# Splitting each 2 MB weight load of a two-block fp32 kernel into two 1 MB loads with a semaphore each

## The chip, the cores and the metric

The kernel runs on one core of a Trainium2 chip. The metric is the device time of one execution in microseconds (us), the median of several runs. Its engines run side by side and meet only at semaphores: PE is TensorE (PEld its weight loads), DVE is VectorE, ACT is ScalarE, POOL is GpSimd, SP is SyncE, which here only issues transfers. Sixteen DMA engines move all data between HBM and SBUF.

## What is computed

Two transformer blocks on 256 tokens of width 1024, all in fp32, batch 1. The first has adaptive modulation, a bidirectional retention with eight heads, a depthwise convolution branch, gates, and a mixture of 32 experts; the second has a gated MLP mixer, a sliding attention, gates and a mixture of 16 experts. Each token goes to two experts. Cut to what matters for the weights:

```python
mod = silu(c) @ w_ada + b_ada                          # 1024 x 6144
q, k, v, g, glu, gates = split(modulate(x) @ w_in + b_in)
ret = silu(g) * head_norm(retention(q, k, v))
y = sigmoid(ga) * (ret @ w_ret_out) + sigmoid(gb) * (conv_branch(glu) @ w_conv_out)
x = layernorm(ALPHA * x + gate * (y @ w_mix_out))
for e in range(32):                                    # 16 in the second block
    h = silu(t @ w_exp_gate[e]) * (t @ w_exp_up[e])    # 1024 x 512 each
    y = y + combine[:, e:e + 1] * (h @ w_exp_down[e])  # 512 x 1024
```

## The kernel before

All weights are cut on the host into blocks of 128 partitions by 4096 fp32 numbers, 16 KB in each partition, 2 MB in all (`BLK`, L41). One block (`kv2`) has half of that, 8 KB in each partition. A block holds a slice of the weights for the whole contraction: for a gate or up matrix and for most dense blocks, columns k*512 to (k+1)*512 of the tile are rows 128k to 128k+127 of the matrix, k from 0 to 7. So the first half of the tile's columns is the first half of the contraction. In a down block it is the first two of four k-tiles of 1024 columns, in `ret` blocks the first 8 of 16.

`make_jobs` (L80) lists every load in the order of use and gives each one of seven bays: three of a ring (`ring`), and four more large tensors (`RA`, `Vc`, `KQ`, `ZC`) that are free of other data in the expert stages. `ROUNDS` (L77) is the order of the bays in each stage: three bays in the dense stage of block one, seven for the experts. SP walks the list (`load`, L334 to L339): it waits until the last job on the block that lay in the bay before is done (`job_done`), and issues one DMA for the whole block, which adds 16 to the bay's semaphore `w_full`. SP's queue is in order.

PE takes the jobs in the same order. `job` (L682) does the dense ones: it waits for `w_full` of the bay (`w_wait`, L297) and for the pair of PSUM banks (`pair_free`), then issues the job's matmuls. The kinds differ in shape: `ada` has 8 matmuls, `cm8` has 4 chunks of 8 k-steps, `tm8` 2 chunks of 8. The first 4 of the 12 `ada` blocks open the kernel: each result goes to DVE (L1125), back through PE (`turn_ada`, L723) and to DVE again (L1106, which adds a slice of `vec` and frees the bank pair). After the fourth, ACT (L442) makes the modulated input `uT`, and the `glu` jobs (L701) begin. ACT issues its own loads meanwhile: `cin`, an early part of `const`, `vec` and the input `xT` at the start (L423 to L427), and after the second `ada` job the rest of `const`, `row`, the context `ctxT` and the router weights (L433 to L437). POOL loads rows of biases (L402).

In the expert stages (`route_and_experts`, L867 on) PE does three jobs for each expert: gate and up (`gate_or_up`, L930) with 16 matmuls of 256 columns each, and down (L945) with 8 of 512 columns. Between them it turns the hidden values and scatters the last expert's output (L920). A matmul in fp32 stands in the trace as two. Thirty experts of block one and fourteen of block two are taken in this static way. The last two, and any second windows of experts with many tokens, run in a loop whose length depends on the data (`Fori`): their loads are issued by `last_experts` (L341, issues at L350 and L357) into three bays with semaphores of their own, `wg_full`, `wu_full`, `wd_full`.

Of the kernel before, what the change touches and what calls it, by code (L numbers as in the profile page):

```python
# [26 lines left out]
ALU = mybir.AluOpType  # L27
# [89 lines left out]
def build(nc, a):  # L117
# [3 lines left out]
    with ExitStack() as ctx:  # L121
# [115 lines left out]
        ld_c, ld_first, ld_rest, ld_x, ld_ctx, ld_wr = (sem(n) for n in ("ld_c", "ld_first", "ld_rest", "ld_x", "ld_ctx", "ld_wr"))  # L237
        w_full = [sem(f"w_full{i}") for i in range(BAYS)]
        job_done = sem("job_done")
# [29 lines left out]
        for n in range(2):  # L269
            moe.append({k: sem(f"{k}{n}") for k in (  # L270
                "logits", "logits_kept", "logits_turned", "gexp_in", "eexp_in", "gexp_out", "eexp_out", "hot_ready", "ranks",
                "items_ready", "u_turned", "u_rows", "diag_ready", "bc_ps", "bc_kept", "wg_full", "wu_full",
                "wd_full", "g_ready", "gathered", "x_kept", "xs_ready", "gate_done", "up_done", "down_done",
                "sg_ready", "hid_ready", "ht_ps", "ht_ready", "y_kept", "s_ready", "scattered", "acc_done", "step")})
# [21 lines left out]

        def w_wait(eng, w):  # L297

            eng.wait_ge(w_full[loads[w]["bay"]], 16 * (loads[w]["nth"] + 1))

# [30 lines left out]
        def _(sp):  # L331
            def load(w):

                x = loads[w]  # L334
                if x["prev"] is not None:
                    sp.wait_ge(job_done, last_of[x["prev"]] + 1)
                s = a["w_" + x["src"]]
                bay = bays[x["bay"]]
                sp.dma_start(bay[:, 0:s.shape[2]], s[x["b"]]).then_inc(w_full[x["bay"]], 16)  # L339

# [80 lines left out]
        def _(act):  # L421
# [154 lines left out]
            def route_and_experts(n):  # L576
# [9 lines left out]
                ins.then_inc(m["u_rows"], 1)  # L586
                act.wait_ge(m["gexp_in"], 1)
                nc.scalar.activation(r_("gd"), r_("gd"), ACT.Exp).then_inc(m["gexp_out"], 1)
                act.wait_ge(m["eexp_in"], 1)
                nc.scalar.activation(r_("e2"), r_("e2"), ACT.Exp).then_inc(m["eexp_out"], 1)  # L590

# [88 lines left out]
        def _(pe):  # L680
            def job(j):

                w_wait(pe, j["w"])
                if j["use"]:
                    pe.wait_ge(pair_free[j["pair"]], j["use"])
                W, out, kind = W_of(j), PP[j["pair"]], j["kind"]
                if kind == "ada":

                    for k in range(DT):
                        at = 32 * (k % 4)  # L690
                        ins = pe.matmul(out[at:at + 32, 0:2, :].rearrange("p a n -> p (a n)"), sT[:, k, :],  # L691
                                        W[:, k * 512:(k + 1) * 512], start=k < 4, stop=k >= 4, tile_position=(0, at))
                elif kind in ("cm8", "cm4", "cm16"):
# [4 lines left out]
                    for c in range(2 if K == 16 else 4):  # L698
                        at = c * P + (512 * j["half"] if K == 4 else 0)
                        for k in range(K):  # L700
                            ins = pe.matmul(out[:, c, :], W[:, k * width + at:k * width + at + P], X[:, k, :],  # L701
                                            start=k == 0, stop=k == K - 1)
                elif kind in ("tm8", "tm8c"):
                    X = ucT if kind == "tm8c" else uT
                    for t in range(LT):
                        for k in range(DT):
                            ins = pe.matmul(out[:, 2 * t:2 * t + 2, :].rearrange("p a n -> p (a n)"),  # L707
                                            X[:, k, t * P:(t + 1) * P], W[:, k * 512:(k + 1) * 512], start=k == 0,
                                            stop=k == DT - 1)
                elif kind == "kv":  # L710
                    for k in range(DT):
                        pe.matmul(out[:, 0, :], W[:, k * 256:k * 256 + P], uT[:, k, :], start=k == 0, stop=k == DT - 1)
                    for t in range(LT):
                        for k in range(DT):
                            ins = pe.matmul(out[:, 2, t * P:(t + 1) * P], uT[:, k, t * P:(t + 1) * P],
                                            W[:, k * 256 + P:(k + 1) * 256], start=k == 0, stop=k == DT - 1)
# [150 lines left out]
            def route_and_experts(n):  # L867
# [56 lines left out]

                def gate_or_up(q, W, x, early=None):
                    for k in range(DT):
                        if early is not None and k % 4 == 0:
                            pe.wait_ge(m["x_kept"], early + k // 4)
# [11 lines left out]

                def down(k, W):
                    pe.wait_ge(m["ht_ready"], k + 1)
                    for c in range(4):
                        for g in range(2):
                            ins = pe.matmul(bank[2][SLOTS * g:SLOTS * (g + 1), :],  # L945
                                            hts[:, c % 2, SLOTS * (c // 2):SLOTS * (c // 2 + 1)],
                                            W[:, c * D + g * 512:c * D + (g + 1) * 512], start=c == 0, stop=c == 3,
                                            tile_position=(0, SLOTS * g))
# [7 lines left out]
                for k in range(E - 2):  # L956
                    jg, ju, jd = (J[f"moe{n}", 3 * k + q, 0] for q in range(3))
                    if k:
                        pe.wait_ge(m["xs_ready"], k)
                    w_wait(pe, jg["w"])  # L960
                    gate_or_up(0, W_of(jg), xs if k else xsc[:, :, 0:SLOTS], None if k else 1).then_inc(job_done, 1)
                    if k == 0:

# [11 lines left out]
                        pe.matmul(flat(MB[3]), ys[:, 0:P], ys, start=True, stop=False)  # L975
                    w_wait(pe, ju["w"])
                    gate_or_up(1, W_of(ju), xs if k else xsc[:, :, 0:SLOTS]).then_inc(job_done, 1)
                    if k:
# [6 lines left out]
                    else:  # L985
                        pe.wait_ge(m["bc_kept"], 1)
                    w_wait(pe, jd["w"])
                    down(k, W_of(jd)).then_inc(job_done, 1)
                wg, wu, wd = (bays[x] for x in tail_bays(n))
# [101 lines left out]
        def _(dve):  # L1091
# [260 lines left out]
            def route(n):  # L1352
# [21 lines left out]
                say(dve, V_.tensor_tensor(t2("gd", GROUPS), lt[:, :, 0:GROUPS], r_("gm").unsqueeze(2).to_broadcast([P, LT, GROUPS]),  # L1374
                                          ALU.subtract), m["gexp_in"], 1)
                first_of(t2("hg", GROUPS), lt[:, :, 0:GROUPS], r_("gm"), GROUPS)
# [10 lines left out]
                link(V_.tensor_reduce(r_("m2"), ml, AX.X, ALU.max))  # L1387
                say(dve, V_.tensor_tensor(r_("e2"), r_("m2"), r_("m1"), ALU.subtract), m["eexp_in"], 1)
                first_of(t2("h2", EG), ml, r_("m2"), EG)
# [5 lines left out]

                dve.wait_ge(m["gexp_out"], 1)
                link(V_.tensor_reduce(r_("gw"), t2("gd", GROUPS), AX.X, ALU.add))
                dve.wait_ge(m["eexp_out"], 1)
                link(V_.scalar_tensor_tensor(r_("w1"), r_("e2"), 1.0, r_("gw"), ALU.add, ALU.mult))
# [329 lines left out]
```

## Time and profile before

| | |
|---|---|
| median of 3 runs | 1634.03 us (1631.02 to 1635.21) |
| the profiled execution | 1630.79 us |
| its span, first to last instruction | 1629.0 us |
| PE busy | 1534.9 us, 94% |
| weight loads (PEld) | 1021.2 us, 63% |
| DVE busy | 492.4 us, 30% |
| ACT busy | 213.7 us, 13% |
| moved by DMA | 435.54 MB, 267 GB/s over the span |
| mean granted TensorE clock | 0.988 of full speed |

The rows in the next section are in microseconds from the first instruction, unless marked ns. A slice of the page is a fortieth of the span, 40.7 us. For a DMA issue, the last number is the time from the issue to the landing of the last byte.

### The profile page before, as it was taken

How to read it: one execution, taken by the hardware profiler on the slowest of the kernel's cores; microseconds unless marked ns; L12 is line 12 of the kernel's file. 1: busy time of each engine (PE TensorE's matmuls, PEld its weight loads, DVE VectorE, ACT ScalarE, POOL GpSimd, SP SyncE). 2: the span in 40 equal slices, each digit the busy share in tenths (PEclk: the TensorE clock that was granted, in tenths of full speed). 3: DMA queues.
4: the chain of work that ended last, by engine and by line, in shares of the span. 5: the costliest groups of instructions: out<-in, count | busy, mean ns of one | idle time of the engine just before them, and what ended most of it. 6: DMA issues, size and time to landing. Idle time of an engine off the chain costs nothing.

```text
span 1629.0 us, 20472 instructions
## 1 busy us (share of the span) xinstructions
PE 1534.9 (94%) x8922; PEld 1021.2 (63%) x8922; DVE 492.4 (30%) x1080; ACT 213.7 (13%) x385; POOL 16.9 (1%) x37
## 2 busy tenths in 40 slices
PE   5999999999999999999998998889999899999996
PEld 2876644674688888555545554547788787555544
DVE  1546686453101117112111111115023133212113
ACT  1100100121112003211111001102022022111102
POOL 0000000000000001000000000000000000000000
PEclk7999999999999999999999999999999999999999
DMA  9523222464433564799999999994544543999994
GB/s 393 197 103 117 104 66 108 169 251 168 150 140 124 193 249 147 286 426 427 427 426 427 425 427 427 427 406 192 142 181 155 207 155 144 426 428 425 427 422 179
DMA packets 33469, 435.54 MB, mean 267 GB/s; under 512 B 4049, under 2 KB 5593, under 8 KB 7145
## 3 DMA queue, kind: packets, MB, share of 16 engines
q1 hardware_dynamic: 29376, 423.64, 64.0%
q10 hardware_dynamic: 2328, 6.15, 1.5%
q0 software_dynamic: 1680, 4.52, 0.8%
q8 instruction: 67, 1.10, 0.3%
q14 instruction: 18, 0.14, 0.0%
HBM read 431.67 MB, written 2.62 MB: 267 GB/s over the span
## 4 chain that ended last, share of the span: by engine, by line
PE 75%; DMA 18%; DVE 3%; ACT 1%; issue 0%; DVEq 0%; SPq 0%; ACTq 0%
PE PP L701 25%; PE PP L930 14%; PE PP L707 13%; PE PP L945 7%; DMA RA<-in_w_moe 6%; DMA ring<-in_w_moe 6%; PE MB L920 4%; DMA Vc<-in_w_moe 4%; DMA ZC<-in_w_moe 2%; PE PP L911 2%; PE MB L849 1%; PE PP L691 1%; PE MB L792 1%; PE MB L774 1%; PE MB L795 1%; PE PP L938 1%
## 5 line engine op out<-in xcount | busy, mean ns | idle before, releaser
L701 PE MATMUL PP<-uT,ring 128*128 128x256 f32 x1088 | 239.4, 382 | 3.7 <-ACT uT L442 2.7
L701 PEld LDWEIGHTS PP<-uT,ring 128*128 128x128 f32 x1088 | 208.0, 192 | 34.4 <-ACT uT L442 2.8
L930 PE MATMUL PP<-ring,const 128*64 128x256 f32 x1312 | 148.8, 380 | 11.5 <-DMA ring<-in_w_moe 10.6
L930 PEld LDWEIGHTS PP<-ring,const 128*64 128x64 f32 x1312 | 98.2, 137 | 68.9 <-DMA ring<-in_w_moe 16.5
L707 PE MATMUL PP<-ring,uT 128*128 128x512 f32 x288 | 125.0, 592 | 0.0
L1477 DVE TENSOR_SCALAR V<-V 128x1 f32<-128x1 f32 x50 | 7.7, 154 | 372.8 <-PE PP L930 372.8
L1164 DVE SCALAR_TENSOR_TENSOR ZC<-ZC,vec 128x256 f32<-128x256 f32 x240 | 116.4, 485 | 8.6
L920 PE MATMUL MB<-V 64*128 64x256 f32 x800 | 112.9, 401 | 1.7 <-DVE V L1488 1.7
L707 PEld LDWEIGHTS PP<-ring,uT 128*128 128x128 f32 x288 | 54.5, 190 | 67.0 <-issue 67.0
L920 PEld LDWEIGHTS MB<-V 64*128 64x128 f32 x800 | 69.1, 186 | 34.5 <-issue 30.0
L707 PE MATMUL PP<-ring,RA 128*128 128x512 f32 x192 | 83.4, 592 | 0.0
L1483 DVE SCALAR_TENSOR_TENSOR V<-V 128x256 f32<-128x256 f32 x100 | 48.5, 485 | 93.0 <-PE MB L920 91.2
L930 PE MATMUL PP<-RA,const 128*64 128x256 f32 x544 | 62.2, 381 | 10.6 <-DMA RA<-in_w_moe 10.2
L945 PE MATMUL PP<-ring,const 128*64 128x512 f32 x304 | 69.4, 598 | 0.0
L607 ACT ACTIVATE V<-PP 128x256 f32<-128x256 f32 x50 | 19.2, 384 | 380.6 <-PE PP L930 380.6
L1488 DVE COPY V<-PP 128x512 f32<-128x512 f32 x50 | 34.6, 692 | 107.2 <-PE PP L945 107.2
L707 PEld LDWEIGHTS PP<-ring,RA 128*128 128x128 f32 x192 | 36.5, 190 | 45.1 <-issue 45.0
L930 PEld LDWEIGHTS PP<-RA,const 128*64 128x64 f32 x544 | 39.4, 137 | 34.9 <-DMA RA<-in_w_moe 13.8
L611 ACT ACTIVATE const<-small 128x512 f32 x50 | 31.8, 636 | 194.5 <-PE PP L930 194.5
L701 PE MATMUL PP<-Vc,ring 128*128 128x256 f32 x256 | 55.6, 379 | 0.0
L930 PE MATMUL PP<-KQ,const 128*64 128x256 f32 x448 | 51.0, 380 | 3.4 <-DMA KQ<-in_w_moe 3.2
L701 PEld LDWEIGHTS PP<-Vc,ring 128*128 128x128 f32 x256 | 48.6, 190 | 6.6
(310 smaller groups left out, 1568.1 us busy)
## 6 DMA issues: line engine op xcount, KB each, us to landing
ring<-in_w_moe SPq DMA_DIRECT2D x61, 2048.0 KB, 23.1
RA<-in_w_moe SPq DMA_DIRECT2D x25, 2048.0 KB, 20.9
ZC<-in_w_moe SPq DMA_DIRECT2D x25, 2048.0 KB, 21.7
KQ<-in_w_moe SPq DMA_DIRECT2D x20, 2048.0 KB, 24.6
Vc<-in_w_moe SPq DMA_DIRECT2D x19, 2048.0 KB, 23.4
ring<-in_w_ada SPq DMA_DIRECT2D x12, 2048.0 KB, 8.7
ring<-in_w_gates SPq DMA_DIRECT2D x7, 2048.0 KB, 8.7
ring<-in_w_v SPq DMA_DIRECT2D x5, 2048.0 KB, 8.4
```

The source lines that it names most:

```text
L607: nc.scalar.activation(sg, bank[0][:, 0:L], ACT.Silu).then_inc(m["sg_ready"], 1)
L611: nc.scalar.activation(xs, xsc[:, :, bass.ds(at, SLOTS)], ACT.Copy).then_inc(m["xs_ready"], 1)
L691: ins = pe.matmul(out[at:at + 32, 0:2, :].rearrange("p a n -> p (a n)"), sT[:, k, :], W[:, k * 512:(k + 1) * 512], start=k < 4, stop=k >= ...
L701: ins = pe.matmul(out[:, c, :], W[:, k * width + at:k * width + at + P], X[:, k, :], start=k == 0, stop=k == K - 1)
L707: ins = pe.matmul(out[:, 2 * t:2 * t + 2, :].rearrange("p a n -> p (a n)"), X[:, k, t * P:(t + 1) * P], W[:, k * 512:(k + 1) * 512], start ...
L911: ins = pe.matmul(out[:, (k % 4) * P:(k % 4 + 1) * P], Kct[:, t, k * P:(k + 1) * P], G[:, c, t, :], start=t == 0, stop=t == 1)
L920: ins = pe.matmul(MB[k // 2][:, k % 2, :], ys[g, (k % 4) * P:(k % 4 + 1) * P], S[g, :], start=False, stop=done == "acc_done" and k % 2 == ...
L930: ins = pe.matmul(bank[q][SLOTS * g:SLOTS * (g + 1), 0:L], x[:, k, :], W[:, k * 512 + g * 256:k * 512 + (g + 1) * 256], start=k == 0, stop ...
L945: ins = pe.matmul(bank[2][SLOTS * g:SLOTS * (g + 1), :], hts[:, c % 2, SLOTS * (c // 2):SLOTS * (c // 2 + 1)], W[:, c * D + g * 512:c * D ...
L1164: ins = V_.scalar_tensor_tensor(conv[:, t, :], zpad[:, t, k:k + L], tap, conv[:, t, :], ALU.mult, ALU.add)
L1483: linked(V_.scalar_tensor_tensor(Sk[:, c], placer[:, c], slotcol, weightr[:, c], ALU.is_equal, ALU.mult), k, c + 2)
L1488: V_.tensor_copy(ys, bank[2]).then_inc(m["y_kept"], 1)
```

## The change

Each block is loaded by two DMAs, one for each half of its columns, and each half has a semaphore of the bay. So a DMA moves 8 KB in each partition, out of rows that lie 16 KB apart in HBM. Every job waits for the first half ahead of its first matmul, and for the second half ahead of the first matmul that reads it, which is the middle of the contraction of its first chunk. The loads of the last experts (`last_experts`) stay whole. To make room for the seven new semaphores, four semaphores of each router are joined to two: `gexp_in` and `eexp_in` become `exp_in` with the values 1 and 2, and the same for `exp_out`.

```diff
-        w_full = [sem(f"w_full{i}") for i in range(BAYS)]
+        w_first = [sem(f"w_first{i}") for i in range(BAYS)]
+        w_second = [sem(f"w_second{i}") for i in range(BAYS)]
...
-        def w_wait(eng, w):
+        def first_half(eng, w):
 
-            eng.wait_ge(w_full[loads[w]["bay"]], 16 * (loads[w]["nth"] + 1))
+            eng.wait_ge(w_first[loads[w]["bay"]], 16 * (loads[w]["nth"] + 1))
+
+        def second_half(eng, w):
+
+            eng.wait_ge(w_second[loads[w]["bay"]], 16 * (loads[w]["nth"] + 1))
...
-                sp.dma_start(bay[:, 0:s.shape[2]], s[x["b"]]).then_inc(w_full[x["bay"]], 16)
+                whole, part = s.shape[2], s.shape[2] // 2
+                sp.dma_start(bay[:, 0:part], s[x["b"], :, 0:part]).then_inc(w_first[x["bay"]], 16)
+                sp.dma_start(bay[:, part:whole], s[x["b"], :, part:whole]).then_inc(w_second[x["bay"]], 16)
...
-                w_wait(pe, j["w"])
+                first_half(pe, j["w"])
...
                         for k in range(K):
+                            if c == 0 and k == K // 2:
+                                second_half(pe, j["w"])
                             ins = pe.matmul(out[:, c, :], W[:, k * width + at:k * width + at + P], X[:, k, :],
                                             start=k == 0, stop=k == K - 1)
...
-                def gate_or_up(q, W, x, early=None):
+                def gate_or_up(q, W, x, early=None, w=None):
                     for k in range(DT):
+                        if w is not None and k == 4:
+                            second_half(pe, w)
...
-                def down(k, W):
+                def down(k, W, w=None):
                     pe.wait_ge(m["ht_ready"], k + 1)
                     for c in range(4):
+                        if w is not None and c == 2:
+                            second_half(pe, w)
...
-                act.wait_ge(m["gexp_in"], 1)
-                nc.scalar.activation(r_("gd"), r_("gd"), ACT.Exp).then_inc(m["gexp_out"], 1)
-                act.wait_ge(m["eexp_in"], 1)
-                nc.scalar.activation(r_("e2"), r_("e2"), ACT.Exp).then_inc(m["eexp_out"], 1)
+                act.wait_ge(m["exp_in"], 1)
+                nc.scalar.activation(r_("gd"), r_("gd"), ACT.Exp).then_inc(m["exp_out"], 1)
+                act.wait_ge(m["exp_in"], 2)
+                nc.scalar.activation(r_("e2"), r_("e2"), ACT.Exp).then_inc(m["exp_out"], 1)
```

The other kinds of dense jobs (`ada`, `tm8`, `kv`) get the same wait at the middle of their k loop, the calls in the expert stages pass the load's number, and DVE's four lines that speak of the joined semaphores follow.

## Rows read from the trace of the kernel before

**Rows 1.** The page's slices of the span: GB/s.
```profile
GB/s 393 197 103 117 104 66 108 169 251 168 150 140 124 193 249 147 286 426 427 427 426 427 425 427 427 427 406 192 142 181 155 207 155 144 426 428 425 427 422 179
```

**Rows 2.** The chain of work that ended last: start, length, what.
```profile
427.87 13.82 PE PP L701 x64
...
518.53 55.27 PE PP L701 x256
...
814.86 30.56 DMA ZC<-in_w_moe
...
1086.38 11.26 DMA RA<-in_w_moe
...
1589.41 10.79 DMA RA<-in_w_moe
```

**Rows 3.** A stretch: length, busy PE, PEld, DVE, ACT, POOL, then PEclk, DMA share, GB/s.
```profile
814.00:1098.00 284.00, 256.32 (x1874) 142.10 (x1872) 50.62 (x114) 27.03 (x58) 0.00 (x0) 1.00 1.00 424
```

**Rows 4.** Two of SP's issues, windows of the DMA view: KB, us to landing.
```profile
Vc<-in_w_moe SPq DMA_DIRECT2D x1, 2048.0 KB, 8.2
...
ZC<-in_w_moe SPq DMA_DIRECT2D x1, 2048.0 KB, 9.8
```

**Rows 5.** Timeline of SP: the issues of rows 4 and 6.
```profile
668.51 0.33 SPq L339 DMA_DIRECT2D Vc<-in_w_moe  x1
...
1093.88 0.44 SPq L339 DMA_DIRECT2D ring<-in_w_q  x1
1094.36 0.53 SPq L339 DMA_DIRECT2D Vc<-in_w_kv  x1
...
1378.95 0.33 SPq L339 DMA_DIRECT2D ZC<-in_w_moe  x1
```

**Rows 6.** A 2 MB block and the 1 MB block queued right behind it.
```profile
ring<-in_w_q SPq DMA_DIRECT2D x1, 2048.0 KB, 23.4
Vc<-in_w_kv SPq DMA_DIRECT2D x1, 1024.0 KB, 25.4
```

**Rows 7.** DMA queues from 21.9 to 29.3: packets, MB, share of 16 engines.
```profile
q1 hardware_dynamic: 142, 2.06, 65.6%
q10 hardware_dynamic: 142, 1.09, 35.4%
```

**Rows 8.** Loads of the start, windows of the DMA view: KB, us to landing.
```profile
hT<-in_xT ACTq DMA_DIRECT2D x1, 1024.0 KB, 27.2
...
ring<-in_w_ada SPq DMA_DIRECT2D x1, 2048.0 KB, 15.0
...
ring<-in_w_glu SPq DMA_DIRECT2D x1, 2048.0 KB, 18.3
const<-in_const ACTq DMA_DIRECT2D x1, 1476.0 KB, 18.5
```

**Rows 9.** Timeline of the start: transfers issued (start of the first, length of all).
```profile
0.73 13.74 SPq L339 DMA_DIRECT2D ring<-in_w_ada  x4
...
2.14 1.11 ACTq L427 DMA_DIRECT2D hT<-in_xT  x1
...
19.28 15.61 SPq L339 DMA_DIRECT2D ring<-in_w_glu  x3
```

**Rows 10.** Timeline of the start: work, and in brackets the idle time before.
```profile
10.39 0.22 ACT L430 ACTIVATE sT<-cin 128x16 f32<-128x16 f32 x1 [5.76 <-DMA cin<-in_cT]
...
16.33 2.91 PE L691 MATMUL PP<-ring,sT 128*32 128x512 f32 x16 [2.26 <-DMA ring<-in_w_ada]
...
21.97 1.42 DVE L1125 COPY small<-PP 128x512 f32<-128x512 f32 x2 [21.97 <-DMA vec<-in_vec]
...
25.13 3.64 PE L691 MATMUL PP<-ring,sT 128*32 128x512 f32 x16 [0.49 <-DVE modT L1106]
...
31.06 3.45 PE L691 MATMUL PP<-ring,sT 128*32 128x512 f32 x16 [0.48 <-DVE modT L1106]
...
39.13 1.22 PE L701 MATMUL PP<-uT,ring 128*128 128x256 f32 x2 [2.71 <-ACT uT L442]
```

More of the change, by code:

```diff
@@ L270, in build @@
             moe.append({k: sem(f"{k}{n}") for k in (
-                "logits", "logits_kept", "logits_turned", "gexp_in", "eexp_in", "gexp_out", "eexp_out", "hot_ready", "ranks",
+                "logits", "logits_kept", "logits_turned", "exp_in", "exp_out", "hot_ready", "ranks",
                 "items_ready", "u_turned", "u_rows", "diag_ready", "bc_ps", "bc_kept", "wg_full", "wu_full",
@@ L689, in job @@
                     for k in range(DT):
+                        if k == DT // 2:
+                            second_half(pe, j["w"])
                         at = 32 * (k % 4)
@@ L700, in job @@
                         for k in range(K):
+                            if c == 0 and k == K // 2:
+                                second_half(pe, j["w"])
                             ins = pe.matmul(out[:, c, :], W[:, k * width + at:k * width + at + P], X[:, k, :],
@@ L706, in job @@
                         for k in range(DT):
+                            if t == 0 and k == DT // 2:
+                                second_half(pe, j["w"])
                             ins = pe.matmul(out[:, 2 * t:2 * t + 2, :].rearrange("p a n -> p (a n)"),
@@ L711, in job @@
                     for k in range(DT):
+                        if k == DT // 2:
+                            second_half(pe, j["w"])
                         pe.matmul(out[:, 0, :], W[:, k * 256:k * 256 + P], uT[:, k, :], start=k == 0, stop=k == DT - 1)
@@ L959, in route_and_experts @@
                         pe.wait_ge(m["xs_ready"], k)
-                    w_wait(pe, jg["w"])
-                    gate_or_up(0, W_of(jg), xs if k else xsc[:, :, 0:SLOTS], None if k else 1).then_inc(job_done, 1)
+                    first_half(pe, jg["w"])
+                    gate_or_up(0, W_of(jg), xs if k else xsc[:, :, 0:SLOTS], None if k else 1, jg["w"]).then_inc(job_done, 1)
                     if k == 0:
@@ L975, in route_and_experts @@
                         pe.matmul(flat(MB[3]), ys[:, 0:P], ys, start=True, stop=False)
-                    w_wait(pe, ju["w"])
-                    gate_or_up(1, W_of(ju), xs if k else xsc[:, :, 0:SLOTS]).then_inc(job_done, 1)
+                    first_half(pe, ju["w"])
+                    gate_or_up(1, W_of(ju), xs if k else xsc[:, :, 0:SLOTS], w=ju["w"]).then_inc(job_done, 1)
                     if k:
@@ L986, in route_and_experts @@
                         pe.wait_ge(m["bc_kept"], 1)
-                    w_wait(pe, jd["w"])
-                    down(k, W_of(jd)).then_inc(job_done, 1)
+                    first_half(pe, jd["w"])
+                    down(k, W_of(jd), jd["w"]).then_inc(job_done, 1)
                 wg, wu, wd = (bays[x] for x in tail_bays(n))
@@ L1374, in route @@
                 say(dve, V_.tensor_tensor(t2("gd", GROUPS), lt[:, :, 0:GROUPS], r_("gm").unsqueeze(2).to_broadcast([P, LT, GROUPS]),
-                                          ALU.subtract), m["gexp_in"], 1)
+                                          ALU.subtract), m["exp_in"], 1)
                 first_of(t2("hg", GROUPS), lt[:, :, 0:GROUPS], r_("gm"), GROUPS)
@@ L1387, in route @@
                 link(V_.tensor_reduce(r_("m2"), ml, AX.X, ALU.max))
-                say(dve, V_.tensor_tensor(r_("e2"), r_("m2"), r_("m1"), ALU.subtract), m["eexp_in"], 1)
+                say(dve, V_.tensor_tensor(r_("e2"), r_("m2"), r_("m1"), ALU.subtract), m["exp_in"], 2)
                 first_of(t2("h2", EG), ml, r_("m2"), EG)
@@ L1394, in route @@
                 say(dve, V_.tensor_tensor(t2("M", E), A[:, 0], A[:, 1], ALU.add), m["hot_ready"], 1)
-                dve.wait_ge(m["gexp_out"], 1)
+                dve.wait_ge(m["exp_out"], 1)
                 link(V_.tensor_reduce(r_("gw"), t2("gd", GROUPS), AX.X, ALU.add))
-                dve.wait_ge(m["eexp_out"], 1)
+                dve.wait_ge(m["exp_out"], 2)
                 link(V_.scalar_tensor_tensor(r_("w1"), r_("e2"), 1.0, r_("gw"), ALU.add, ALU.mult))
```

## The prediction

> **What bounds the kernel now.** I read the page's slices first. PE is busy nearly everywhere, but the transfers have two plateaus at 422 to 428 GB/s, slices 18 to 26 and 35 to 39, and far less outside [rows 1]. A plateau at one height is a limit, so the next question is who sets the end in it. The chain of waits answers: it runs over PE until 814.86, and from there steps on weight transfers, 30 us long at first, come again and again to the end of block one's experts; block two's experts end the same way [rows 2]. In the table of stretches, 814 to 1098 has a DMA share of 1.00 at 424 GB/s, and PE idles 28 us [rows 3].
>
> The point to see is that the transfers set the end of each expert stage from well before 814. A transfer issued at 668.51 lands 8.2 us later [rows 4, 5], and a block takes 2.097 MB / 424 GB/s = 4.95 us, so it already stood behind another. PE has prefetched blocks and so does not feel it until it has eaten them. But the last block lands when all bytes since 668 have been moved, whatever PE does. It lands at 1086.38 + 11.26 = 1097.64 [rows 2]. Block two does the same from the transfer that was issued at 1378.95 and landed at 1388.7 [rows 4, 5], to 1589.41 + 10.79 = 1600.2 [rows 2]. Elsewhere PE sets the pace and loads have slack, but for the first 39 us, where loads, DVE and PE take turns [rows 10].
>
> So the change has two prices that can show: what a block costs the DMA engines in the two full stretches, and what happens in the first 39 us.
>
> **Part 1: the waits it shortens in the expert stages.** PE can start a gate job 2.45 us sooner once the first half has landed. It then stops at the middle for the second half. The wait is about 1 us a block and there were 28 us of it from 814 to 1098 [rows 3]. It is worth nothing at the end: the transfer ahead does not come sooner, because the queue is never empty (share 1.00, and 30 us from issue to landing, six blocks deep [rows 2, 3]). The last experts' loads, the ones that do end the stage, stay whole and have their old waits. Gain 0.
>
> **Part 2: the price of smaller packets.** A block is 128 rows of 16 KB, and becomes 256 rows of 8 KB and a second round of semaphore writes. The trace has two rows with 8 KB pieces. The lower bound is `kv2`, 1 MB from the same queue right behind `q2`: they land at 1094.36 + 25.4 = 1119.76 and 1093.88 + 23.4 = 1117.28 [rows 5, 6], 2.48 us for 1 MB with times rounded to 0.1. The same bytes at 424 GB/s take 2.47. With the rounding, two such halves cost between 0 and 0.1 us more than a whole block; I take 0.03 as the low end. The upper bound is from 21.9 to 29.3, where ACT's queue q10 moves `xT` in 8 KB pieces beside q1's 16 KB pieces. q1 spends 0.656 * 16 * 7.4 / 2.06 = 37.7 us of one engine on a MB, q10 0.354 * 16 * 7.4 / 1.09 = 38.5 [rows 7]. The difference of 0.8 us a MB is 0.8 * 2.097 / 16 = 0.10 us a block, 0.13 if the last digit of the shares falls badly. I take 0.06, nearer to `kv2`, since that row is of the same queue and back to back.
>
> How many blocks pay? In block one, from the landing at 668.51 + 8.2 = 676.7 to 1097.64 there are 421 us, 85 blocks at 4.95, with the first 86; five of these are whole ones of the last experts, so 81. In block two, 211.5 us are 43 blocks, 11 of them whole, so 32. 113 * 0.06 = +6.8 us; the ends give 113 * 0.03 = 3.4 and 113 * 0.13 = 14.7. Before 668, and between the stages, the loads are asked for long ahead and the price is hidden by PE's own work.
>
> The Trainium skill (DMA: Bandwidth & Descriptors, section Bandwidth) speaks against the change: its table has 1 MB transfers at 6.15 us, 78% of peak, and asks for at least 1 MiB. By that figure, with nothing overlapped, 226 halves would add 226 * (6.15 - 2.48), some 830 us; this trace disagrees, since the 1 MB block passes in 2.48 us. The same section's paragraph on small descriptors gives 3 cycles of 850 MHz for each packet: an estimate from it is 8 * 3.5 ns = 0.03 us a block and a total of +3.2 us, the low end above.
>
> **Part 3: the start.** At the start the two queues take turns packet by packet, and not by bytes. ACT's queue has `cin`, `const`, `vec` and `xT`, each in 128 rows. The small `cin` lands at 10.39 and the small `vec`, two places on, only at 21.97, though SP's second `ada` block is there at 16.33 [rows 10]: that is one place of ACT's queue for each block of SP's. `xT` (1 MB) lands at 2.14 + 27.2 = 29.3 with SP's fourth block (0.73 + 13.74 + 15.0 = 29.5), and the rest of `const` at 19.3 + 18.5 = 37.8 with the first `glu` block, 19.28 + 18.3 = 37.6 [rows 8, 9]. With 8 KB pieces on SP's queue, an ACT transfer will land with one half of a block, so SP's share falls. 1 MB is 2.45 us. Taking it out of each step (10.4, then 5.9, 5.6 and 7.4 us): `cin` 7.9, `const` and the whole first block 11.5, `vec` 14.7 with half of the second block, `xT` and the second block 19.7 (before 16.33). PE ends the second `ada` job 1.7 us (its last four k-steps) later, 21.4 (before 16.33 + 2.91 = 19.2 [rows 10]). That job releases ACT's second set of loads. `vec` no longer holds the turn, so the third job starts at 23.8 (before 25.13) and ends near 27.4 (before 28.8). But from 23.5, about 2 us after ACT's issues, the third and fourth blocks share the engines with 1.48 MB of `const`, then `row` and `ctxT`. Half a block beside `const` takes the step from 29.5 to 37.6 less 2.45, 5.7 us, where before the fourth block had only `xT` beside it. The halves of the third block land at 22.2 and 25.5, those of the fourth near 30.5 and 34.4. So the fourth job ends at 34.4 + 1.7 = 36.1 (before 31.06 + 3.45 = 34.5), and 4.6 us later the `glu` jobs start, at 40.7 (before 39.13). The first `glu` block's second half lands near 41.5 to 42, after its first four k-steps (1.7 us), which adds little. I take +2.0 us. Bounds: -1.5, if ACT's loads do not delay the fourth block (third job 1.3 us sooner, and all behind it); +4, if the first `glu` block is late as well. The shift passes whole through the PE-bound stretch and into both expert stages.
>
> **Part 4: what costs nothing.** Sixty dense jobs get a wait in the middle that is already met. The waits met at the head of a job show no cost: one `cm8` job is 13.82 us, and four in a row 55.27 [rows 2]; at most 0.01 each, 0.6 in all. SP issues twice as often, 0.33 to 0.53 us each [rows 5], two within 4.95 us, and with nothing else on its queue but loads. Behind a PE wait in the middle stand only that job's own matmuls. The joined semaphores count the same two events on ACT and DVE in the same order: 0.
>
> **Sum.** 0 + 6.8 + 2.0 + 0 = +8.8 us. The profiled execution took 1630.79 us around its span of 1629.0 and would take 1639.6; it stands 3.2 us under the median, so the median goes from 1634.0 to 1642.8, call it 1643 (+0.54%). About 0.3%, 4.9 us, is what a measurement of this kernel can tell from no change.
>
> **The rivals.**
> *The packets are almost free.* 0.03 us a block or less and a start of 0 to +1: 1634 + 3.4 + 0.5 = 1638, a change that can't be told. For it speaks `kv2`; against it the dearer 8 KB pieces of rows 7 and the extra semaphore writes. Chance 0.22.
> *The shorter waits pay.* If SP's issues, and not the engines, held the stream, PE's earlier release of a bay (up to 1.8 us, half a job) would move every later transfer. It would take back PE's idle time: 28 us in 814 to 1098 and, scaled by length to the 75 us that end block two's experts, 7 more: at most 1634 - 35 + 2 = 1601, and it decides as soon as the DMA share between 700 and 1098 is under 1.00 by more than 4.9 / 430 of it. The share of 1.00 and the 30 us in the queue are against it [rows 2, 3]. Chance 0.10, with smaller gains of any kind in it.
> *Small transfers cost more than a packet's share.* With 12 or 14 transfers in flight instead of 6 or 7 the engines may lose time between them, or the 16 KB stride reads slower from HBM; the trace has no such row. A transfer that met one other in the queue landed in 8.2 us where its bytes need 4.95 [rows 4]; if a tenth of that 3.2 showed for each added transfer, it would be 113 * 0.32 = +36, and 1634 + 36 + 2 = 1672. Chance 0.08. (The table of the Trainium skill cited in part 2, DMA: Bandwidth & Descriptors, Bandwidth, points this way.)
> *The forecast.* 1643, its own range 1638.5 to 1649. Chance 0.60.
>
> **How the numbers follow.** The range leaves out the large gain, the 1672 case and slivers, and takes in the free packets and both bounds of part 2: 1631 to 1650. Slower: 0.60 less a sliver, 0.08, and a fifth of the first rival: 0.68. Same: 0.21. Faster: 0.11.
>
> **What would show it.** In the changed profile: the plateaus at 420 to 423 GB/s where they had 424 to 427, the share still 1.00; the `glu` jobs starting at 40 to 42 with `vec` landed near 15 and the second `ada` block near 20; PE's waits for DMA more in number and shorter; last landing of block one some 8 us after 1097.64. It would be wrong if the plateaus keep their height, if they fall below 418, or if the DMA share in them drops under 1.

## The result and the profile after

The changed kernel takes 1645.14 us in the median of 4 runs (1641.72 to 1647.64), the kernel before 1632.85 us in the median of its 4 (1631.02 to 1635.21; one run more than in the table above). The ratio is 1.0077, 95% interval 1.0060 to 1.0093: slower, by more than the 0.3% that a measurement of this kernel can tell. The profiled execution took 1641.72 us around a span of 1639.9, against 1630.79 and 1629.0: +10.9 us on either count.

The page's slices of the changed kernel, GB/s, and two rows of its queues and issues:

```profile
GB/s 387 199 103 116 103 66 107 171 249 163 153 150 108 205 256 125 308 419 420 420 421 420 420 420 420 420 405 200 155 166 154 205 154 154 421 419 420 422 417 182
...
q1 hardware_dynamic: 55872, 423.65, 64.4%
...
ring<-in_w_moe SPq DMA_DIRECT2D x114, 1024.0 KB, 24.7
```

The plateaus stand where they stood, but their height is 417 to 422 GB/s instead of 422 to 428 [rows 1]. The load of one block has become two issues of 1 MB, and queue q1 has 55872 packets for the 29376 of before, for the same 424 MB.

The chain of waits of the changed kernel (start, length, what):

```profile
1026.22 29.91 DMA RA<-in_w_moe
...
1094.71 11.21 DMA RA<-in_w_moe
...
1600.31 10.84 DMA RA<-in_w_moe
```

The last up block of block one lands at 1094.71 + 11.21 = 1105.92, where it was 1097.64; that of block two at 1611.15, where it was 1600.20 [rows 2]. The start of the changed kernel, in its timeline:

```profile
10.56 1.93 PE L700 MATMUL PP<-ring,sT 128*32 128x512 f32 x8 [2.36 <-DMA ring<-in_w_ada]
...
14.00 1.93 PE L700 MATMUL PP<-ring,sT 128*32 128x512 f32 x8 [1.51 <-DMA ring<-in_w_ada]
14.17 0.69 DVE L1144 COPY small<-PP 128x512 f32<-128x512 f32 x1 [14.17 <-DMA vec<-in_vec]
...
18.97 1.93 PE L700 MATMUL PP<-ring,sT 128*32 128x512 f32 x8 [3.04 <-DMA ring<-in_w_ada]
...
29.11 1.94 PE L700 MATMUL PP<-ring,sT 128*32 128x512 f32 x8 [0.48 <-DVE modT L1125]
...
32.92 1.94 PE L700 MATMUL PP<-ring,sT 128*32 128x512 f32 x8 [1.88 <-DMA ring<-in_w_ada]
34.79 3.58 PE L738 MATMUL PP<-const,small 128*128 128x2 f32 x16
...
41.07 9.29 PE L712 MATMUL PP<-uT,ring 128*128 128x256 f32 x31 [2.71 <-ACT uT L449]
```

An `ada` job is now two groups of 8 matmuls. `vec` lands at 14.17 (21.97 before), but the second half of the second block only at 18.97 (the whole at 16.33 before), and the fourth job stands in its middle for a half that lands at 32.92. The `glu` jobs begin at 41.07 instead of 39.13 [rows 10].

With three events in each trace (first `glu` matmul, last up block of block one, last up block of block two) the loss can be placed: 1.94 us up to the first event, 1064.85 - 1058.51 = 6.34 us from the first to the second, 505.23 - 502.56 = 2.67 us from the second to the third. These are called the start, the first stretch and the second stretch below. The sum is 10.95 us, all of the profile's difference. The 113 split blocks that stand in a full queue pay 9.0 / 113 = 0.080 us each.

This is one pair of executions. How far another pair could differ is read from the others: with whole blocks in the expert stages the first stretch took 1057.41 to 1058.87 us in five kernels (the one before and four of the experiments below), so differences of up to 1.5 us in it say nothing.

### The profile page after: what moved, and what is told of

The parts are those of the page before. It is cut to its first block, busy times and chain, and to the rows that moved or that the text cites. A ratio compares the mean times of both kernels' runs of the same rounds, so it can differ in the third digit from the quotient of the medians.

```text
span 1639.9 us, 20658 instructions
## 1 busy us (share of the span) xinstructions
PE 1544.3 (94%) x8922; PEld 1013.8 (62%) x8922; DVE 492.0 (30%) x1080; ACT 213.6 (13%) x385; POOL 16.7 (1%) x37
## 3 DMA queue, kind: packets, MB, share of 16 engines
q1 hardware_dynamic: 55872, 423.65, 64.4%
q10 hardware_dynamic: 2328, 6.15, 1.5%
## 4 chain that ended last, share of the span: by engine, by line
PE 70%; DMA 24%; DVE 3%; SPq 1%; ACT 1%; issue 1%; DVEq 0%; ACTq 0%
PE PP L712 25%; PE PP L720 13%; DMA RA<-in_w_moe 12%; PE PP L947 11%; PE PP L964 5%; DMA KQ<-in_w_moe 3%; DMA ring<-in_w_moe 3%; PE MB L935 3%; DMA ring<-in_w_ada 2%; PE PP L926 2%; DMA Vc<-in_w_moe 2%; DMA ZC<-in_w_moe 2%; PE MB L864 1%; PE PP L700 1%; PE MB L807 1%; PE MB L789 1%
## 5 line engine op out<-in xcount | busy, mean ns | idle before, releaser
L947 PE MATMUL PP<-ring,const 128*64 128x256 f32 x1312 | 152.2, 381 | 12.7 <-DMA ring<-in_w_moe 12.5
L947 PEld LDWEIGHTS PP<-ring,const 128*64 128x64 f32 x1312 | 93.9, 137 | 76.5 <-DMA ring<-in_w_moe 27.0
```

The source lines that it names most:

```text
L947: ins = pe.matmul(bank[q][SLOTS * g:SLOTS * (g + 1), 0:L], x[:, k, :], W[:, k * 512 + g * 256:k * 512 + (g + 1) * 256], start=k == 0, stop ...
```

## The experiments

The first question was what in a split block costs 0.08 us: its smaller packets, the second transfer, or the 16 KB stride in HBM. The second was whether the start is a separate cost. The third came from the rival of the shorter waits. All edits are against the changed kernel, except the last experiment's.

**Halves contiguous in HBM.** The static experts' weights come from a second copy.

```diff
-                sp.dma_start(bay[:, 0:part], s[x["b"], :, 0:part]).then_inc(w_first[x["bay"]], 16)
-                sp.dma_start(bay[:, part:whole], s[x["b"], :, part:whole]).then_inc(w_second[x["bay"]], 16)
+                h = a["h_" + x["src"]]          # [block, 2, 128, 2048]; dense blocks keep the two lines above
+                sp.dma_start(bay[:, 0:part], h[x["b"], 0]).then_inc(w_first[x["bay"]], 16)
+                sp.dma_start(bay[:, part:whole], h[x["b"], 1]).then_inc(w_second[x["bay"]], 16)
...
+        d[f"h_moe{n}"] = np.ascontiguousarray(s.reshape(3 * E, P, 2, BLK // 2).transpose(0, 2, 1, 3))
```

> The expert blocks of the static experts are loaded in two transfers as in the changed kernel, but from a second copy of the weights in which each half lies contiguous in HBM (8 KB rows behind one another), so the 16 KB stride is gone and all else is as in the changed kernel. In the changed kernel the first glu job starts at 41.07 (before 39.13), the last up block of block one lands at 1105.92 (before 1097.64) and that of block two at 1611.15 (before 1600.20): 1.94 us are lost at the start, 6.35 in block one's expert stage and 2.66 in block two's, 9.0 for 113 blocks, 0.080 us each. Theory packets (each packet and each semaphore write has a fixed price): landings within 0.7 us of 1105.9 and 1611.2. Rival stride (HBM reads at a 16 KB pitch are slower): landings near 1099.6 and 1602.2, a gain of 9 us on the changed kernel. Rival transfers (each DMA has a price, or the issue that SP is held in): as theory packets.

Measured: 1644.51 us, ratio 1.0075 (1.0054 to 1.0097), plateaus at 420 GB/s, `glu` jobs from 41.53, landings at 1107.00 and 1614.96. The first stretch is 1065.47 us, as in the changed kernel and not 6 us less. The stride costs nothing that can be seen. The landings are 1.1 and 3.8 us past the changed kernel's, more than the 0.7 that was forecast: the `glu` jobs began 0.5 us later, and of the second difference 2.7 us arise in PE's middle stage, where the granted clock fell (below).

**Halves by partitions, lower and upper.**

```diff
-                sp.dma_start(bay[:, 0:part], s[x["b"], :, 0:part]).then_inc(w_first[x["bay"]], 16)
-                sp.dma_start(bay[:, part:whole], s[x["b"], :, part:whole]).then_inc(w_second[x["bay"]], 16)
+                sp.dma_start(bay[0:half, 0:whole], s[x["b"], 0:half, :]).then_inc(w_first[x["bay"]], 16)
+                sp.dma_start(bay[half:P, 0:whole], s[x["b"], half:P, :]).then_inc(w_second[x["bay"]], 16)
```

> Two transfers of 1 MB again with a semaphore each, but cut by partitions: rows 0 to 63 and rows 64 to 127, 16 KB in each. PE waits for both ahead of a job. Number of transfers, semaphore writes and SP's issues as in the changed kernel, packets as in the kernel before. Theory packets: the two expert stages cost 0 to 1.5 us together (113 semaphore writes an engine), the glu jobs start at 38 to 39.5, span 1629 to 1631. Rival transfers: the stages cost 9.0 us, span near 1638. Rival stride: 0.

Measured: 2226.43 us, ratio 1.3663 (1.3578 to 1.3749). Every theory missed this one. Its row of 900 to 1000, with the columns of rows 3:

```profile
900.00:1000.00 100.00, 61.37 (x344) 35.11 (x344) 9.24 (x22) 5.49 (x12) 0.00 (x0) 0.80 1.01 218
```

The DMA engines are busy all the time (1.01) and move 218 GB/s, half. So transfers into one half of the partitions keep all engines busy and get half of the rate, and this experiment says nothing about the price of a transfer as such. The even and odd partitions, below, took its place.

**Only the start split, and all but the start.** In the first, the condition below; in the second, `w >= 8`. PE's wait for the second half has the same condition.

```diff
+                if w < 8:
                     sp.dma_start(bay[:, 0:part], s[x["b"], :, 0:part]).then_inc(w_first[x["bay"]], 16)
                     sp.dma_start(bay[:, part:whole], s[x["b"], :, part:whole]).then_inc(w_second[x["bay"]], 16)
+                else:
+                    sp.dma_start(bay[:, 0:whole], s[x["b"]]).then_inc(w_first[x["bay"]], 16)
```

> Only the first eight loads (four ada, four glu) are split, all others are whole as before. Theory (at the start the queues take turns by packets, so ACT's large loads take more of the engines beside 8 KB packets and the fourth ada block is late): glu jobs start at 41.1, both expert stages cost 0, span 1631 (+1.9), time +0.12%. Rival (the start in the changed profile was the clock or chance, and all 10.9 us are the stages): glu jobs start at 39.1, span 1629.

> The complement: the first eight loads are whole, all later ones split. Theory: glu jobs start at 39.1, stages cost 6.35 + 2.66 = 9.0 us, span 1638, time +0.55%. Rival: the whole 10.9 us, span 1640.

Measured, start only: 1634.66 us, ratio 1.0020 (1.0010 to 1.0030), `glu` jobs from 41.47, first stretch 1057.41 (none of the 6.3 us), plateaus back at 427 GB/s. Its span is 1633.0 and not 1631, for the second stretch is 505.38 although no block in it is split. Measured, all but the start: 1643.03 us, ratio 1.0066 (1.0043 to 1.0090), first stretch 1064.97, span 1640.3 and not 1638; here too the second stretch is long, 508.32. So the two parts are separate and come near to the whole.

The start of this second version was forecast at 39.1, as in the kernel before, and began 0.9 us earlier:

```profile
30.96 1.92 PE L706 MATMUL PP<-ring,sT 128*32 128x512 f32 x16 [0.48 <-DVE modT L1131]
...
38.20 6.10 PE L718 MATMUL PP<-uT,ring 128*128 128x256 f32 x15 [3.40 <-DMA ring<-in_w_glu]
```

Its first eight loads are the ones of the kernel before. But its fourth `ada` job took 1.92 us at a granted clock of 1.00, where the kernel before took 3.45 at 0.53 [rows 10], and PE then waited for the first `glu` block. So the kernel before had a slow start in its profile, and the price of the start is not fixed: 1.9 us against that profile, about 3 against this one.

What else the forecasts missed by is the middle of the second stretch. Its windows from 1180 to 1230, of the kernel before, of the start-only kernel, of the changed one and of its complement:

```profile
1180.00:1230.00 50.00, 47.29 (x270) 41.95 (x269) 11.70 (x17) 11.30 (x14) 4.47 (x8) 1.00 0.50 189
```
```profile
1180.00:1230.00 50.00, 47.29 (x256) 41.75 (x255) 11.69 (x17) 11.30 (x14) 4.39 (x8) 0.93 0.45 169
```
```profile
1180.00:1230.00 50.00, 47.29 (x268) 41.86 (x267) 11.69 (x17) 9.30 (x12) 4.29 (x8) 1.00 0.50 186
```
```profile
1180.00:1230.00 50.00, 47.29 (x253) 41.63 (x252) 11.70 (x17) 9.20 (x11) 4.28 (x8) 0.93 0.44 167
```

The granted clock is 1.00 in the kernel before and in the changed one, and 0.93 in the two experiments: around the attention, where PE has waits for DVE between its jobs, the clock falls to 1.2 GHz for a moment in some executions. In the start-only kernel it averages 0.65 from 1210 to 1215, and PE gets through 16 matmuls there and not 25. With it goes 2.8 us (505.38 against 502.56, both with whole blocks in the second stretch). Corrected by that, the complement's second stretch is 508.32 - 2.8 = 505.5, as in the changed kernel. The correction is itself rough: the last experiment below has whole blocks, reads 0.93 too, and took 507.38. The first stretch has no such stage, and its spread is 1.5 us, so the verdicts below go by it.

**One transfer, small packets.** 2 MB in one DMA with one semaphore, but 8 KB pieces, for the static experts; the dense blocks are whole, in 16 KB pieces.

```diff
+                    sp.dma_start(bay.rearrange("p (h n) -> p h n", h=2), h[x["b"]].rearrange("h p n -> p h n")
+                                 ).then_inc(w_first[x["bay"]], 16)
```

> One transfer of 2 MB for each block with one semaphore, as before, but the static experts' blocks come from the copy with the halves apart in HBM, so that each packet is 8 KB: 256 packets a transfer. Packets of the changed kernel without its second transfer. Stage costs are read between events inside a run: from the first glu matmul to the landing of the last up block of block one (1058.51 before, 1064.85 changed), and from there to the landing of the last up block of block two (502.56 and 505.23; these hold PE's middle stage, where a dip of the granted clock can add 2 to 3 us). Theory packets: most of the price stays, 1063.5 to 1064.8 us in the first stretch, since only one semaphore write in 18 goes. Rival transfers: 1058.5. SP's issues fall back to 0.3 to 0.5 us in either case.

Measured: 1640.62 us, ratio 1.0068 (1.0042 to 1.0095), first stretch 1101.62 - 37.90 = 1063.72, plateaus at 420 GB/s. Of the 6.3 us in this stretch 5.2 are there with half of the transfers; the 1.1 that are missing are within the spread. The `glu` jobs began at 37.90, with whole blocks at the start as in the version above. The forecast on SP was wrong: its issues did not fall back to 0.5 us (one of them, of `KQ` at 1015.23, took 3.15), see the last section.

**Even and odd partitions.** The counterpart: two transfers, two semaphores, 16 KB packets, PE waiting for both.

```diff
+                sp.dma_start(bay[0:P:2, 0:whole], s[x["b"], 0:P:2, :]).then_inc(w_first[x["bay"]], 16)
+                sp.dma_start(bay[1:P:2, 0:whole], s[x["b"], 1:P:2, :]).then_inc(w_second[x["bay"]], 16)
```

> Two transfers of 1 MB and two semaphores as in the changed kernel, PE waiting for both, each of 64 rows of 16 KB, but the even and the odd partitions instead of the lower and the upper half, where the rate had halved (217 GB/s). Theory A, each transfer covers every part of SBUF and the rate is back: with 16 KB packets the first stretch is 1058.5 to 1060 and the plateaus are at 424 to 427 GB/s, against 1064.9 if the price were one of transfers. Theory B, any transfer of 64 rows is slow: near 217 GB/s and 2200 us as with the halves of partitions.

Measured: 1636.71 us, ratio 1.0030 (1.0016 to 1.0044), first stretch 1099.62 - 40.26 = 1059.36. Theory A: the rate is back at 427 GB/s, and 81 added transfers cost at most 0.85 us, 0.01 each, which the spread of 1.5 us does not tell from nothing. The rest of its 3.8 us is the start (+1.1) and the second stretch (+1.8, clock 0.97 there). The stretch 900 to 1000 in four kernels, first the one with one transfer and 8 KB packets, then even and odd, then the changed kernel, then quarters:

```profile
900.00:1000.00 100.00, 88.06 (x654) 49.83 (x652) 16.68 (x37) 8.80 (x19) 0.00 (x0) 1.00 1.01 420
```
```profile
900.00:1000.00 100.00, 89.61 (x664) 53.48 (x661) 16.87 (x39) 8.96 (x20) 0.00 (x0) 1.00 1.01 427
```
```profile
900.00:1000.00 100.00, 91.28 (x646) 46.75 (x644) 17.97 (x40) 8.81 (x19) 0.00 (x0) 0.98 1.01 420
```
```profile
900.00:1000.00 100.00, 87.54 (x638) 44.64 (x632) 16.68 (x37) 8.82 (x19) 0.00 (x0) 1.00 1.03 409
```

The last number is what the reader is to see: 420 with one transfer or with two, as long as the packets are 8 KB, and 427 with two transfers of 16 KB packets. The packets make the price.

One rival is left by this comparison: in the changed kernel, with one transfer of 8 KB pieces and with quarters, SP was also held at its issues (last section), and in the even and odd one it was not. The changed kernel's own trace decides it. From 683 to 764 all its issues took 0.33 to 1.05 us, and the rate was already down, here from 680 to 760, first before, then changed:

```profile
680.00:760.00 80.00, 80.00 (x604) 44.40 (x602) 16.53 (x37) 8.44 (x18) 0.00 (x0) 1.00 1.01 427
```
```profile
680.00:760.00 80.00, 80.00 (x600) 44.09 (x598) 16.89 (x38) 8.44 (x18) 0.00 (x0) 1.00 1.01 420
```

**Quarters.** The suspected cost tripled.

```diff
+                for i in range(4):
+                    n = s.shape[2] // 4
+                    sp.dma_start(bay[:, i * n:(i + 1) * n], s[x["b"], :, i * n:(i + 1) * n]
+                                 ).then_inc((w_first, w_second)[i // 2][x["bay"]], 16)
```

> The suspected cost tripled: every static block in four transfers of 512 KB, 4 KB in each partition, the first two on the first semaphore and the last two on the second (32 in each wait). Theory packets: 24 packets and 3 semaphore writes more an engine than before, where the change had 8 and 1, so three times its 0.080 us a block: +0.24 * 81 = +19 in the first stretch (1078) and +0.24 * 32 = +8 in the second (510). The start gets worse as well, since ACT's transfers then land with a quarter of a block each: glu jobs at 42 to 45. Span near 1660. Rival, a price by transfer or by SP's issue that only shows when SP is held: more than four times, span over 1675.

Measured: 1667.96 us, ratio 1.0234 (1.0208 to 1.0260). First stretch 1122.61 - 45.62 = 1076.99 (forecast 1078), second 512.79 (forecast 510), `glu` jobs from 45.62 (forecast 42 to 45). 409 GB/s is 5.13 us a block, 420 is 4.99 and 427 is 4.91: 8 more packets and one more semaphore write an engine cost 0.08 us, 24 and 3 cost 0.22. So a packet, with its share of a semaphore write, costs about 9 to 10 ns of an engine on top of its bytes.

**PE waits for both halves.** The early start on the first half is taken away.

```diff
         def first_half(eng, w):
             eng.wait_ge(w_first[loads[w]["bay"]], 16 * (loads[w]["nth"] + 1))
+            eng.wait_ge(w_second[loads[w]["bay"]], 16 * (loads[w]["nth"] + 1))
...
         def second_half(eng, w):
-            eng.wait_ge(w_second[loads[w]["bay"]], 16 * (loads[w]["nth"] + 1))
+            pass
```

> The changed kernel's transfers, but PE waits for both halves ahead of a job, so the early start on the first half is taken away. Theory (the early start is worth nothing where transfers set the pace, and at the start only the fourth ada job's half, 1.9 us): first stretch 1064.9 as changed, last landings where they were but for the start, glu jobs at 42 to 43.5, span 1641 to 1643. Rival (the shorter waits paid, and the price of transfers is larger than 9 us): span over 1650.

Measured: 1644.57 us, ratio 1.0081 (1.0059 to 1.0104), the changed kernel's. `glu` jobs from 41.92, first stretch 1065.53, span 1642.8. PE's waits for the ring's blocks from 814 to 1098 (in total, times, longest), before, changed, and with both halves waited for:

```profile
PE PP L930 <- DMA ring<-in_w_moe: 10.6, 11, 1.1
```
```profile
PE PP L947 <- DMA ring<-in_w_moe: 10.4, 24, 0.6
```
```profile
PE PP L948 <- DMA ring<-in_w_moe: 13.2, 14, 2.2
```

For the ring's blocks the split halves the longest wait and doubles the number. Over all bays the sum of PE's waits for blocks is 26.1 us before, 27.0 with the split and 31.1 with both halves waited for, and the longest with the split is 2.1, one for `RA`. The end of the stage stays in all of them where the stream puts it.

**Three blocks split, ACT's loads later.** What the runs point to: split only where small packets help, at the start, and keep ACT's large loads away from the fourth `ada` block. The first of the three versions is below; the other two also issue `xT` after the third `ada` job, and the last of them has no split at all.

```diff
+                if w < 3:
                     sp.dma_start(bay[:, 0:part], s[x["b"], :, 0:part]).then_inc(w_first[x["bay"]], 16)
...
-            job_wait(act, J["ada", 1, 0])
+            job_wait(act, J["ada", 3, 0])
             act.dma_start(const[:, early:], a["const"][:, early:]).then_inc(ld_rest, 16)
```

> A version made from what the runs show: only the first three ada blocks are split, since there the 8 KB packets let ACT's small loads through (vec at 14.2 where it was 22.0); the fourth and all others are whole; and ACT's second set of loads (const's rest, row, ctxT, router weights) is issued after the fourth ada job, not the second, so that nothing delays the fourth block. Theory: fourth ada block lands near 29, glu jobs start at 37.3 (before 39.13), or up to 1 us off with the granted clock; expert stages as before; span 1627, time -0.1%. Rival (the context load becomes late for ACT and delays the glu results' way out of PSUM): glu jobs start at 37.3 but 1 to 3 us are lost before 111; span 1629 to 1631.

> As e9, and the input xT (1 MB) is issued after the third ada job, not at the start: it is needed only for the first glu job. Theory: ada blocks land 2.4 us sooner, glu jobs start near 35, span 1625, time -0.25%. Rival (xT lands beside the first glu block and becomes what the glu jobs wait for): glu jobs start at 37 or later.

> The control to e10: the kernel before with all blocks whole and the same two delays of ACT's loads. Theory (with 16 KB packets vec still lands with the third ada block, near 22, and the turn of the first ada result waits for it): glu jobs start at 38.5 to 39.1, time within 0.1% of before. Rival (the delays alone do the work, the split nothing): glu jobs start near 35 to 36.

First `glu` matmul of the three:

```profile
36.03 24.22 PE L718 MATMUL PP<-uT,ring 128*128 128x256 f32 x99 [2.71 <-ACT uT L455]
```
```profile
38.12 22.24 PE L719 MATMUL PP<-uT,ring 128*128 128x256 f32 x93 [4.20 <-ACT uT L456]
```
```profile
41.45 18.90 PE L702 MATMUL PP<-uT,ring 128*128 128x256 f32 x78 [7.65 <-ACT uT L443]
```

The first starts the `glu` jobs 3.1 us earlier than the kernel before (and 1.9 to 2.2 earlier than the two versions with whole blocks above) and keeps it to the last up block of block one (1094.27 against 1097.64). In its profile the clock in the middle stage was 0.93 and the second stretch 505.33 us instead of 502.56, which took 2.8 of it: span 1628.4, and 1630.69 us against 1631.62, ratio 1.0006 (0.9994 to 1.0018). That is no difference. The second fell to its rival: `xT`, issued at 23.9, is 12.0 us under way beside SP's blocks and holds ACT to 35.99; 1630.52 us, ratio 1.0001 (0.9990 to 1.0012). In the third, with whole blocks, it lands at 39.24 and costs 2.3 us; 1635.44 us, ratio 1.0024 (1.0011 to 1.0038). Neither its theory (38.5 to 39.1, time unchanged) nor its rival came true: the `glu` jobs wait for the late `xT`, which lands 3.3 us later than in the second version. No version that was run beats the kernel before by what can be measured.

## Why the prediction was right, step by step

The way, the two prices and their order were right, and the median of 1645 lies near the 1643 of the forecast. The rise itself was put too low: +8.8 us against 10.9 in the profiles and 12.3 in the medians.

**What bounds the kernel** held: both expert stages end with the byte stream. Taking PE's early start away again moves the first stretch by nothing that can be told (1064.85 to 1065.53 us), and slowing the stream by small packets alone, with one transfer, lengthens it (1058.51 to 1063.72).

**Part 1, the shorter waits, 0:** right. The waits became more and mostly shorter, and removing the benefit changed the time by nothing that can be measured (ratios 1.0077 and 1.0081).

**Part 2, smaller packets, +6.8 us:** the mechanism was right, the size too small. It measured 9.0 us. The count of 113 blocks holds: the price of a block by the rates alone, 4.99 - 4.91 us, is the same 0.08 as by the landings. The term that was mis-sized is that price, 0.080 us instead of 0.06. The measured value lies between the two bounds, `kv2`'s 0.03 and the 0.10 to 0.13 of `xT`'s row; the choice was set too near the lower one. That bound was drawn too tight. 2.48 us is a difference of two times that are each rounded to 0.1, so it is good to 0.1 either way, and two such halves against a whole block to 0.2: the row could not tell 0 from 0.2 us, and so not 0.03 from 0.08. The upper one is wider too, 0.05 to 0.14 us with the rounding of the megabytes. The Trainium skill's estimate from 3 cycles a packet (DMA: Bandwidth & Descriptors, Bandwidth) was 0.03 us a block; the runs show 0.08. Its 6.15 us for a transfer of 1 MB is measured on another path, issued from GpSimd, and does not carry over: in SP's full queue 420 GB/s are 2.50 us for 1 MB.

**Part 3, the start, +2.0 us:** +1.94 us, and +2.3 with only the start split. The turn-taking by packets came as worked out (`vec` at 14.2 for 14.7, the second block at 19.0 for 19.7). But the close agreement of the sum is luck, for two errors cancel in it: the fourth job ended at 34.9 and not at 36.1, and from there to the `glu` jobs it took 6.2 us and not 4.6, since the last turns (L738) took 3.58 us where they had taken 1.99. That is TensorE's lower clock. The row of the granted clock reads 1.00 for these turns in the changed kernel, but the version with contiguous halves and the one that waits for both took 3.57 and 3.58 us for them with the clock at 0.50. It is no chance of one execution either: with all four `ada` blocks split by columns, all five kernels took 3.57 or 3.58, and PE had waited 1.9 to 4.8 us inside or before the fourth job. With whole blocks at the start it was 1.98 or 1.99 in four of four. Why the clock is low there is not shown: the even and odd version waited 3.3 us before its fourth job and took 1.99. And the start of the kernel before was itself slow in the profile that both the sum and the +1.94 go by; against 38.2 and 37.9 in the two other kernels whose start is unchanged, the split start costs some 3 us. The ratio of the start-only kernel, 1.0020 (1.0010 to 1.0030), is 1.6 to 4.9 us.

**Part 4, waits and issues at nothing:** right for PE and the semaphores within what can be told: the first stretch of the even and odd version, with 81 blocks of two transfers, is 0.85 us longer in all. For SP it was right in effect and wrong in fact: its issues took up to 6.3 us, but the queue behind them was never empty (share 1.01), and the rate was down before the first of them was held.

The sum was +8.8 us; the profiled executions differ by 10.9, the medians by 12.3, with an interval that reaches from 9.8 to 15.2 us by the ratio. Of what is missing, 2.2 us are the price of a block. The rest may in part be the clock. In 47 more runs of the kernel before, the 14 with a mean granted clock of 0.985 to 0.987 took 1633.6 us on average and the 18 with 0.991 to 0.994 took 1629.8, so a kernel's executions differ by several us that go with the clock. The changed kernel's profiled execution reads 0.995, its other three 0.988 to 0.992 with times of 1643.03 to 1647.64. How much of the difference of the medians is the clock, and how much a price that the profiled pair hides, as at the start, stays open.

## What to carry to other kernels

When the DMA share is 1.00 over a stretch, the transfers' own efficiency is the term to look at, and splitting a load makes it worse by its added packets: here 427, 420 and 409 GB/s at 16, 8 and 4 KB pieces. A consumer that starts on the first half gains nothing there, since the stream's last byte sets the end. Where two queues share the engines, count rows and not bytes: a small load lands sooner when the other queue's pieces are small, and a large one on the other queue then takes a larger share of the engines.

## What the hardware showed that was not expected

**Half of the partitions, half of the rate.** Transfers of 64 rows into partitions 0 to 63 or 64 to 127 moved 218 GB/s with the engines busy all the time; the same 64 rows into even or odd partitions 427 GB/s. The Trainium skill explains it (SBUF — State Buffer, the section on the DMA port swizzle): the rate depends on how many of SBUF's 16 ports the partitions reach, and bit 6 of the partition's number picks between the two ports of each pair, so that partitions 0 to 63, or 64 to 127, reach 8 and the even or the odd ones all 16. This case's two runs agree, with 218 and 427 GB/s.

**SP is held when many rows are queued.** Issues of the changed kernel at 1026.22, 1034.76 and 1036.93, and of the even and odd version at 1020.63 and 1021.14:

```profile
1026.22 6.32 SPq L346 DMA_DIRECT2D RA<-in_w_moe  x1
...
1034.76 2.13 SPq L346 DMA_DIRECT2D ZC<-in_w_moe  x1
1036.93 2.12 SPq L345 DMA_DIRECT2D Vc<-in_w_moe  x1
```
```profile
1020.63 0.47 SPq L346 DMA_DIRECT2D RA<-in_w_moe  x1
1021.14 0.60 SPq L347 DMA_DIRECT2D RA<-in_w_moe  x1
```

An issue took 0.33 us before. It is not the number of transfers in flight that holds SP: the even and odd version has as many and goes free. With r rows an engine and one semaphore write, the queue's depth is the time from issue to landing over the time of a transfer, times r + 1. From the medians between 900 and 1000 this is 27.6 / 2.5 * 9 = 99 entries for the changed kernel, 31.3 / 5.0 * 17 = 106 for one transfer with 8 KB packets, and 15.1 / 1.28 * 9 = 106 for quarters. The versions that are not held have 30.9 / 4.9 * 9 = 57 (before) and 29.0 / 2.46 * 5 = 59. The changed kernel's first held issue, at 768.25, gives a lower figure: loads issued then land in 25.0 us, 90 entries by the same sum, and those issued at 764.4 to 766, not held, in 23.5 us, 85. So a queue seems to take some 85 to 106 entries an engine before the issuer waits; that is an inference from these numbers, the limit itself was not tried.

**The clock in the middle stage.** The second stretch, with the same whole blocks, took 2.8 us more in two executions where the granted clock from 1180 to 1230 was 0.93 of full instead of 1.00, 4.8 in a third, and 1.7 in one at 0.97. This is as large as the effects that were looked for; comparing event to event inside each trace kept it out of the first stretch.
